# The first half's query and gate tiles by seven products of quarters, and the output weight's sums moved beside the attention

## The reference

```python
z = rms_norm(h, norm_gain)
proj = z @ w_in                      # q 1024, k 128, v 128, g_attn 1024, u_pool 1024, g_pool 1024
q, k = partial_rotary(q), partial_rotary(k)
o_attn = chunked_window_attention(q, k, v, sinks)   # chunks of 64: own + previous chunk + meta tokens
o_pool = multiscale_pool_mixer(u_pool, w_pool, pool_scale)   # windows 2, 4, 8, 16
h = h + concat([silu(g_attn) * o_attn, silu(g_pool) * o_pool]) @ w_out
return rms_norm(h, final_norm_gain)[:, N_META:]
```

## Time and profile before

| | us |
|---|---|
| median of 3 runs | 1237.42 (1236.21 to 1237.77) |
| profiled execution | 1239.35 |
| its span, first to last instruction | 1237.5 |
| TensorE busy | 1219.3 (99% of the span) |
| VectorE busy | 816.7 (66%) |
| ScalarE busy | 582.6 (47%) |
| POOL busy | 173.3 (14%) |

### The profile page before, as it was taken

The page is one execution under the profiler, slowest core; times in us unless marked ns, Lnnn a source line. Parts: engine busy times, 40 slices in busy tenths (PEclk is TensorE's granted clock), DMA queues, the critical chain, the costliest instruction groups (busy, mean ns, idle before and its releaser), DMA issues.

```text
span 1237.5 us, 16662 instructions
## 1 busy us (share of the span) xinstructions
PE 1219.3 (99%) x6017; PEld 985.8 (80%) x6017; DVE 816.7 (66%) x1291; ACT 582.6 (47%) x1372; POOL 173.3 (14%) x227
## 2 busy tenths in 40 slices
PE   9899999999999999999999999999999999999997
PEld 9788888877777777788888888887777777788886
DVE  6544553456575757967676976657766676695757
ACT  7532222255555555444755334334555555544455
POOL 1156776300000000500001000000000000200000
PEclk9999999999999999999999999999999999999999
DMA  9536556411111101963244423336111111253324
GB/s 361 205 105 241 197 212 220 162 68 35 35 34 34 35 34 35 363 224 119 86 171 170 136 69 119 103 128 238 37 44 40 34 35 35 84 206 102 119 88 167
DMA packets 46319, 152.57 MB, mean 123 GB/s; under 512 B 4656, under 2 KB 8272, under 8 KB 46256
## 3 DMA queue, kind: packets, MB, share of 16 engines
q1 hardware_dynamic: 29328, 90.45, 21.3%
q0 software_dynamic: 16928, 61.25, 13.6%
HBM read 119.70 MB, written 35.91 MB: 126 GB/s over the span
## 4 chain that ended last, share of the span: by engine, by line
PE 91%; DVE 4%; issue 2%; ACT 2%; DMA 1%; DVEq 0%; ACTq 0%; POOL 0%; POOLq 0%
PE ps L1425 16%; PE ps L1427 16%; PE ps L1426 16%; PE ps L1724 8%; PE ps L1726 7%; PE ps L1725 7%; PE ps L1616 3%; PE ps L1696 2%; PE ps L1670 2%; PE ps L1600 2%; PE ps L1601 2%; PE ps L1602 2%; DMA xr<-in_x 1%; PE ps L1698 1%; DVE wsplit L985 1%
## 5 line engine op out<-in xcount | busy, mean ns | idle before, releaser
L1425 PE MATMUL ps<-zh,wsplit 128*128 128x512 f32 x912 | 360.6, 395 | 0.3 <-DVE gates_all L1092 0.2
L1427 PE MATMUL ps<-zh,wsplit 128*128 128x512 f32 x912 | 356.3, 391 | 0.0
L1426 PE MATMUL ps<-zl,wsplit 128*128 128x512 f32 x912 | 355.9, 390 | 0.0
L985 DVE TENSOR_TENSOR wsplit<-wraw,wsplit 128x1024 fp32r<-128x1024 f32 (+1 forms) x132 | 169.3, 1283 | 117.3 <-ACT wsplit L655 95.1
L1427 PEld LDWEIGHTS ps<-zh,wsplit 128*128 128x128 f32 x912 | 171.5, 188 | 36.7
L1425 PEld LDWEIGHTS ps<-zh,wsplit 128*128 128x128 f32 x912 | 171.7, 188 | 35.6 <-DVE gates_all L1092 1.3
L1426 PEld LDWEIGHTS ps<-zl,wsplit 128*128 128x128 f32 x912 | 171.8, 188 | 34.2
L1724 PE MATMUL ps<-wsplit,gsh 128*128 128x512 f32 x448 | 174.6, 390 | 1.9 <-DVE gsl L1330 1.7
L1725 PE MATMUL ps<-wsplit,gsh 128*128 128x512 f32 x448 | 174.3, 389 | 0.0
L1726 PE MATMUL ps<-wsplit,gsl 128*128 128x512 f32 x440 | 171.2, 389 | 0.0
L655 ACT ACTIVATE wsplit<-wraw 128x1024 fp32r<-128x1024 f32 x112 | 119.6, 1068 | 95.1 <-PE ps L1726 66.4
(11 more groups left out here) (224 smaller groups left out, 1692.8 us busy)
## 6 DMA issues: line engine op xcount, KB each, us to landing
wraw<-wt SPq DMA_DIRECT2D x32, 512.0 KB, 3.3
wraw<-in_wa SPq DMA_DIRECT2D x26, 512.0 KB, 3.9
wraw<-in_wq SPq DMA_DIRECT2D x24, 512.0 KB, 3.6
wraw<-wat SPq DMA_DIRECT2D x17, 512.0 KB, 3.2
tq<-in_wq POOLq DMA_DIRECT2D x8, 1024.0 KB, 6.6
wt<-tq POOLq DMA_DIRECT2D x8, 1024.0 KB, 5.6
wraw<-wc SPq DMA_DIRECT2D x16, 512.0 KB, 3.3
wraw<-in_wb SPq DMA_DIRECT2D x16, 512.0 KB, 3.5
```

What stands on the lines that cost most here:

```text
L985: ve.tensor_tensor(wl[:, slot, 0:size], wraw[:, slot, 0:size], wh[:, slot, 0:size].bitcast(F32), ALU.subtract).then_inc(w_lo, 1)
L1425: te.matmul(ps[:, PB[bank], :], w_h, rhs_z(zh, tb, k), start=k == 0, stop=False)
L1426: te.matmul(ps[:, PB[bank], :], w_h, rhs_z(zl, tb, k), start=False, stop=False)
L1427: last = te.matmul(ps[:, PB[bank], :], w_l, rhs_z(zh, tb, k), start=False, stop=k == KT - 1)
```

## The change

- The first half takes the second half's form of stage 2: `Fori` loops over eight pairs become three plain pairs and the stream of 35 products, on every engine; token sums, `gstage`, `gd`, `za` and the reordered first attention step with them.
- POOL makes the weight sums of pairs 3 to 7 first, one pair after the other, each after the stores of the last have landed. Its buffers are now slices 7 and 8 of `qk` (runs of 64 numbers), and ScalarE waits for all five pairs before it copies product 7 of pair 5 into one of them.
- Products 1 to 3 read `wa` itself; the fifteen copies into `wat` are gone, and a block of the stream is two loads of 256 KB, in both halves.
- The output weight's sums go from the eight steps in stage 2 to sixteen steps of half the size in the first half's stage 3, each behind a copy of keys; the last ends behind the last copy, ahead of `gsl_first`. SP waits for them before the output product's third factor, as before.
- In the first half's first attention step TensorE waits for the last gate tile's bank ahead of `project_meta`.

The diff, cut to its core (counters that only change their numbers are left out):

```diff
@@ memory @@
-    wat = nc.dram_tensor("wat", (NBLK, P, 2, TB), F32, kind="Internal").ap()
+    wat = nc.dram_tensor("wat", (HT - PAIR0, 4, P, TB), F32, kind="Internal").ap()
...
-        tq = at(r_at, "tq", [P, 4, TB])
+        tq, _ = place("tq", [P, 4, TB // 2])
+        ta_g, ta_q = qk[:, :, HT - 1, :], qk[:, :, HT, :]
+        def weight_of(j, prod):
+            if prod > 3:
+                return wat[j - PAIR0, prod - 4]
+            return wa[(2, 2, 3)[prod - 1] + 2 * j, :, (0, TB, TB)[prod - 1]:(0, TB, TB)[prod - 1] + TB]
@@ SP, now for both halves @@
-                    sp.wait_ge(ta_out, 16 * 4 * (HT - PAIR0))
-                    sp.wait_ge(wat_out, 16 * 3 * (HT - PAIR0))
-                    for b in range(NBLK):
-                        halves = min(2, NPROD - 2 * b)
-                        load(block_s(b), b % 2, wat[b, :, 0:halves, :], size=halves * TB)
-                        gates_behind(b)
+                for b in range(NBLK):
+                    sp.wait_ge(w_lo, block_s(h, b) - 1)
+                    for half, (jj, prod) in enumerate(STREAM[2 * b:2 * b + 2]):
+                        if prod > 3:
+                            sp.wait_ge(ta_out, 16 * 4 * (jj + 1))
+                        sp.dma_start(wraw[:, b % 2, half * TB:half * TB + TB], weight_of(PAIR0 + jj, prod)).then_inc(ws_in[b % 2], 16)
+                    gates_behind(b)
@@ POOL, first half @@
+                    composed(pool)
+                    for jj in range(HT - PAIR0):
+                        pair = PAIR0 + jj
+                        if jj > 0:
+                            pool.wait_ge(ta_out, 16 * 4 * jj)
+                        for there, tile in ((ta_q, 2 + 2 * pair), (ta_g, 3 + 2 * pair)):
+                            gp.dma_start(there, chunks(wa[tile])).then_inc(ta_in, 16)
+                        b12, b22, b11, b21 = (part[:, half * NCH // 2:(half + 1) * NCH // 2, :] for part in (ta_g, ta_q) for half in range(2))
+                        pool.wait_ge(ta_in, 32 * (jj + 1))
                         for i, (o, a, b) in enumerate(((b11, b12, b11), (b12, b22, b12), (b22, b22, b11), (b21, b21, b22))):
                             gp.tensor_tensor(o, a, b, ALU.subtract).then_inc(ta_step, 1)
+                            pool.wait_ge(ta_step, 4 * jj + i + 1)
+                        for prod, part in ((7, b12), (6, b22), (4, b21), (5, b11)):
+                            gp.dma_start(chunks(weight_of(pair, prod)), part).then_inc(ta_out, 16)
...
+                    pool.wait_ge(x_done, NPROD)
+                    quarters_in(0)
+                    for c in range(2, NCH):
+                        window_keys(c // 2, c % 2)
+                        quarters_sum(c - 2)
+                        quarters_in(c - 1)
+                    quarters_sum(NCH - 2)
+                    quarters_in(NCH - 1)
+                    quarters_sum(NCH - 1)
...
-                if h == 0:
-                    for j in range(PAIR0, HT):
-                        for prod, tile, rows_half in ((1, 2 + 2 * j, 0), (2, 2 + 2 * j, 1), (3, 3 + 2 * j, 1)):
-                            gp.dma_start(wat_at(j, prod), wa[tile, :, rows_half * TB:rows_half * TB + TB]).then_inc(wat_out, 16)
@@ ScalarE, the stream @@
+                        act.wait_ge(x_done, NPROD * h + q + 1)
+                        if h == 0 and prod == 7 and j == HT - 3:
+                            act.wait_ge(ta_out, 16 * 4 * (HT - PAIR0))
+                        there = z_keep(j) if prod == 7 else queries(j, 0 if prod == 1 else 1)
@@ VectorE, ScalarE and TensorE alike @@
-                if h == 0:
-                    with dve.Fori(0, HT) as j:
-                        pair_a(j)
-                else:
...
+                for j in range(PAIR0):
+                    pair_a(j, [[s_sums[i] for i in places] for places in SUMS[j]])
@@ TensorE, first attention step @@
-                        if h > 0 and g == 0 and sub == 0:
+                        if g == 0 and sub == 0:
                             project(slot, 0, 0, 3)
                             pe.wait_ge(rot_done, (1 + HT) * (h + 1))
...
                         if h == 0 and sub < 2:
+                            if g == 0 and sub == 0:
+                                pe.wait_ge(pb_free[0], FREES * h + HT + CREDIT)
                             pe.wait_ge(m_ev, 2 + 2 * g + sub)
                             project_meta(slot)
```

More of the change, by code:

```diff
@@ L237, in build @@
         p_gate = sem("p_gate")
-        ta_in, ta_step, ta_out, wat_out = sem("ta_in"), sem("ta_step"), sem("ta_out"), sem("wat_out")
+        ta_in, ta_step, ta_out = sem("ta_in"), sem("ta_step"), sem("ta_out")
+        ws_in = [sem(f"ws_in{i}") for i in range(2)]
         za_out, za_back = sem("za_out"), sem("za_back")
@@ new lines, in _ @@
+                for i in range(1, 1 + PAIR0):
+                    for slot in range(2):
+                        load(block_a(h, 2 * i + slot), slot, wa[2 * i + slot])
+                    if i == 1:
+                        sp.wait_ge(z_hi, NTT * (h + 1))
+                        sp.wait_ge(z_lo, NTT * (h + 1))
+                        for part, z in enumerate((zh, zl)):
+                            sp.dma_start(za[part].rearrange("p t (k c) -> p t k c", c=P), quarter(z, 1, 0).bitcast(F32)).then_inc(za_out, 16)
+                    if i >= 3:
+                        gates_out(i - 3)
@@ L452, in _ @@
-                with sp.Fori(h, NG) as g:
+                for r in range(2):
+                    load(block_b(h, 0, r), r, wc[0, r])
+                    gates_behind(NBLK + r)
+                sp.wait_ge(g_out, 16 * (HT - 1) * (h + 1))
+                sp.wait_ge(x_done, NPROD * h + place_of(HT - 1, 6) + 1)
+                gates_back(0)
+                sp.wait_ge(x_done, NPROD * h + place_of(HT - 1, 5) + 1)
+                for part, z in enumerate((zh, zl)):
+                    sp.dma_start(quarter(z, 1, 0).bitcast(F32), za[part].rearrange("p t (k c) -> p t k c", c=P)).then_inc(za_back, 16)
@@ L453, in _ @@
+                gates_back(1)
+                for r in range(2):
+                    load(block_b(h, 0, 2 + r), r, wb[0, r])
+                gates_back(2)
+                gates_back(3)
+                with sp.Fori(1, NG) as g:
                     for r in range(2):
@@ L601, in _ @@
                 window_keys(0, 1)
-                with pool.Fori(1, NCH // 2) as pair:
-                    for slot in range(2):
-                        window_keys(pair, slot)
+                if h == 0:
+                    pool.wait_ge(x_done, NPROD)
[7 more added lines that the diff above has]
+                    quarters_sum(NCH - 1)
+                else:
+                    with pool.Fori(1, NCH // 2) as pair:
+                        for slot in range(2):
+                            window_keys(pair, slot)
                 pool.wait_ge(s_done, NCH * (h + 1) + CREDIT)
@@ L1571, in pair_a @@
                     gate_tile(j)
+                for j in range(1, PAIR0):
+                    pair_a(j)
+                pe.wait_ge(v_tok, h + 1)
                 if h == 0:
-                    with pe.Fori(1, HT) as j:
-                        pair_a(j)
-                else:
-                    for j in range(1, PAIR0):
-                        pair_a(j)
-                    pe.wait_ge(v_tok, HALVES)
+                    pe.wait_ge(vm_done, 1)
+                    pe.wait_ge(m_ev, 2)
+                else:
@@ L1638, in bank_free @@
                         def bank_free(tb, ahead=0):
-                            if h > 0 and g == 0 and sub == 0 and not ahead:
+                            if g == 0 and sub == 0 and not ahead:
                                 return
```

383 lines of the change are left out of this document (158 added, 225 removed).

## The result

The changed kernel takes 1251.39 us in the median of 4 runs (1249.8 to 1257.2), the kernel before 1237.6: a ratio of 1.0119 [1.0083, 1.0155]. It is slower by 1.2%, 14 us, where 5 us faster was forecast, and it lies outside the range given. The profiled execution took 1257.2 us, the longest of the four.

The account below looks back on a forecast made before the run. The prediction took TensorE, busy 99% of the span, as the bound. It summed -11.6 + 4.5 + 2.0 + 0 + 0 = -5.1 us, off the median of 1237.42: 1232.3 us, range 1225 to 1249.

Parts of the forecast that it names:

- What goes, -11.6 us: First half: 60 matmuls fewer with the second half's waits, -10.8 us, and a shorter first attention step, -0.8 us.
- the -0.8 us: First attention step, from last tile to second scores: 16.2 us before, 15.4 after the reordering.
- The rival in which POOL and VectorE pass by each other: In the first half the two engines don't collide: -11.6 us alone, 1225.8 us; chance 0.14.
- VectorE and POOL, +6.5 us: First half, shared SBUF access: POOL's subtractions delay VectorE, +3 at gate tile 0, +1.5 at gate tile 1, +2.0 in the stream.
- The weight sums, 0: Five pairs' sums on POOL: last store lands at 181.7 us (168 to 257), just in time, cost 0.
- The deadline: ScalarE's wait before copying product 7 of pair 5: last weight sum needed at 177.5 us, 183 with TensorE's earlier losses.
- loads 7.0: POOL's weight sums: loading 1 MB a pair was taken as 7.0 us, low 5.7, high 14.
- stores 6.0: POOL's weight sums: four stores of 256 KB a pair were taken as 6.0 us, low 4.5, high 14.
- Sixteen steps beside the attention, 0: First half's stage 3: output weight's sums take 7.2 us a step, between key copies 14.5 to 16.2 us apart; cost 0.
- 3.4 us in hand: First output step: `gsl_first` ends at 491.6 us, and anything up to 495.0 is free.
- The third rival: POOL late at the output stage: with its DMAs at 6.5 us, +5 us, 1237.3 us; chance 0.08.
- The first rival: Weight sums late at ScalarE's wait, released by a DMA: each microsecond after 183 lost on TensorE, 1236 to 1260; chance 0.30.

Follow-up runs that it names:

- experiment 4: The changed kernel with POOL's twenty weight subtractions left out, loads and stores kept (products 4 to 7 use wrong weights): 1227.55 us.
- experiment 1: The changed kernel with product 7 of pairs 5 and 6 kept in a separate buffer, so ScalarE's wait comes nine products later: 1232.12 us.
- experiments 2: The changed kernel with pair 3's weight sums made early, at 49 us, before POOL's first cosine product: 1230.19 us.
- 8: Changed kernel, pair 3's sums early, `gsl_first` earlier, 512-byte runs: 1229.49 us; also products kept elsewhere and pair 4's loads held until gate tile 0 left its bank: 1228.28.
- the control: The changed kernel itself, unedited, run again beside the kernel with runs of 512 bytes: 1252.04 us.
- experiment 7: The changed kernel with weight-sum buffers in runs of 512 bytes, profiled twice more: 1242.38 and 1234.42 us.
- experiment 6: The changed kernel with the weight-sum buffers laid over columns 7 and 8 together, in runs of 512 bytes instead of 256: 1242.73 us.

## Why the prediction was wrong

- **What goes, -11.6 us: right in sum, by luck in one term.** Without POOL's subtractions the first half is 9.8 us shorter than before (161.1 + 400.5 against 170.7 + 400.7), and the late `gsl_first`, 2.0 us, is still in that: -11.8. The five pairs' stream takes 97.8 us (98.0 predicted, 108.8 plain): -11.0, and so gates by way of `gd` and quarters by `za` cost nothing, as taken. But the first attention step got no shorter. TensorE's rows, of the kernel before and of experiment 4:

```profile
246.59 0.39 PE L1427 MATMUL ps<-zh,wsplit 128*128 128x512 f32 x1
...
261.95 1.25 PE L1616 MATMUL ps<-kw,qk 64*128 64x144 f32 x16
...
232.90 0.39 PE L1599 MATMUL ps<-s4h,wsplit 128*128 128x512 f32 x1
...
248.54 1.25 PE L1613 MATMUL ps<-kw,qk 64*128 64x144 f32 x16
```

  From the end of the last tile to the second scores are 15.1 us before and 15.4 after. The 16.2 of the prediction came from an edge at 245.8, set by counting matmuls; the tiles end at 246.8, since the plain loop has gaps of 1.0 us in sum, nearly all at two borders of pairs (115.5 and 137.8 us). The new form has none of these. So the -0.8 us was the wrong place for a gain of about that size. The rival in which POOL and VectorE pass by each other gave 1225.8; 1227.55 less 2.0 is 1225.6.
- **VectorE and POOL, +6.5 us: the mechanism right, the size some two to three times too large.** The lock costs 1.1 us an instruction, as taken. By the Trainium skill ("SBUF — State Buffer", on the shared port pair) one instruction waits for the whole of the other; the trace agrees in size, 1.05 to 1.10 us each beside subtractions of 1.3 us alone. At gate tile 0 the gate product came 3.3 us late (3 predicted), but the slack was 1.3 us, not zero, so TensorE waited 1.9. At gate tile 1 it was 0 to 0.9 in most executions and 1.7 in the one of experiment 1 (1.5 predicted), in the stream about 0.4, and 1.0 more in experiment 1 (2.0 predicted). Together 2.3 us, 3.8 where the clock fell: the tiles of experiments 2 and 8 against 4.
- **The weight sums, 0: this step failed.** The deadline (183 predicted, 182.5 measured) was right and the subtractions a little less than taken (41 and 38.1); "loads 7.0" was 8.8 and "stores 6.0" was 9.0. Three things were under-sized. The run of 256 bytes was put at 12 ns an engine by a line through runs of 1 and 4 KB; it takes 19, which is 1.8 us more for each MB, and the stores had been given nothing for it but issue. That is extrapolation beyond the last point. The landing after the last issue was taken as the median of one store (2.9 us, 4.9 now), where four are in flight. And SP's loads beside them were left out: the next load waited 4.2 to 8.0 us after the end of the issues, longest where SP moved most. Times five that is 20.3 us late with nothing in hand. Measured directly, the late sums are the difference of the tiles between the control and experiment 2, 21.7 us: 18.1 of wait, the rest mostly the half clock behind it.
- **Sixteen steps beside the attention, 0: a small miss.** Scores don't wait. But 3.4 us in hand were none: a store took 4.6 to 4.9 us from issue to the next load (3.3 taken), a load 4.5 (4.3) and four subtractions 3.2 (2.8), so `gsl_first` ended 31.9 us after the last copy of keys instead of 27.5. 1.4 to 1.8 us of wait, 2 to 4 us with the clock. The third rival, too, was real in part.
- **The sum.** -11.8 + 2.3 + 21.7 + 2.2 = +14.4 us, which is what lies between the marks of before and of the control. The terms are differences of these same marks, so that they add up is no check of them; that each sits where it is said to is shown by the edits.

The first rival had the place, the sign, the releaser and, with 1246 us at 3 us more a pair, nearly the size. Its chance of 0.30 was too small: "it just meets the deadline" for a chain of fifteen pieces, ten of them loads and stores whose run length no row had, with bounds of 168 and 257 for a deadline of 183, leaves far more room for a miss than for a gain. The half clock stood in no term.

## What to carry to other kernels

When a chain of loads, sums and stores runs against a fixed wait, count it pair by pair with the landing of the last of several DMAs in flight, not the median of one; and where the result is "just in time", ask first whether the wait can be put later or the chain earlier. Here either alone turned 1.2% slower into 0.5 to 0.6% faster, with no work saved. A wait on a buffer placed ahead of the engine's other duties costs all that is queued behind it: nine products later the same late store cost TensorE nothing.

## What was not expected of the hardware

- After a wait TensorE's clock may be at half speed. In waits of 18 to 20 us it fell to 0.50 (1.2 GHz) and read that up to the end of the wait and some 4 to 5 us beyond, matmuls 0.43 us apart instead of 0.23. After a wait of 1.8 us at the first output step it read 0.50 for 6 us. The same length doesn't always do it: behind a wait of 1.93 us at gate tile 0 the clock fell in the kernel after (0.51 from 98 to 100 us), and behind one of 1.94 us at the same place in experiment 2 it stayed at 1.00; behind 1.4 us at the first output step it fell in the control, behind 1.8 us in the quicker execution of experiment 7 it didn't. What decides that, these runs leave open.
- A DMA issued by POOL occupies it for 0.55 us with 128 runs, 0.75 with 512, 0.88 with 1024 and 1.16 with 2048 (means of the issue rows).
- The DMA engines take about 9 ns for a run on top of its bytes, from 2 KB down to 256 bytes alike (experiment 6): a run of 256 bytes takes 19 ns where its bytes alone would take 10 at the 412 GB/s of the earlier trace rows.
